# Keys, queries, the recurrent norm's sum, then values: a new sequence in the mixer of a two-layer hybrid network

## What is computed

```python
z = rms_norm(h, mix_pre_g[l]) @ w_in[l]
xr, gr, cq, ckv, kr = jnp.split(z, splits, axis=-1)
y_lru = rglru_group(xr, gr, ...)              # conv, two gates, a scan over tokens, times gelu(gr)
q  = (rms_norm(cq, q_norm_g) @ w_uq)          # 8 heads of 64 + 32 (rope)
kv = (rms_norm(ckv, kv_norm_g) @ w_ukv)       # 8 heads: 64 of key, 64 of value
k_rope = apply_rope(kr, cos[None], sin[None]) # shared by the heads
y_mla = causal_block_attention(qf, kf, v)
y = jnp.concatenate([rms_norm(y_lru, lru_out_g[l]), rms_norm(y_mla, mla_out_g[l])], axis=-1) @ w_out[l]
h = h + rms_norm(y, mix_post_g[l])
```

## Time and profile before

| quantity | value |
|---|---|
| median of 3 executions | 2087.74 us (2084.95 to 2088.3) |
| profiled execution, its own time | 2087.94 us |
| its span, first to last instruction | 2086.1 us |
| PE busy | 2050.4 us, 98% of the span |
| POOL, ACT, DVE busy | 1061.0, 767.5, 729.4 us (51%, 37%, 35%) |
| DMA queue of the weights | 25.9% of 16 engines |
| chain that ended last | PE 89%, POOL 4%, DVE 3%, issue 2%, ACT 1% |
| TensorE clock granted, mean | 0.995 |

### The profile page before, as it was taken

How to read it: one execution, slowest core, us unless ns; L and a number is a source line. 1 busy time by engine, 2 the same in 40 slices (tenths; PEclk the granted TensorE clock), 3 DMA queues, 4 the chain that set the end, 5 groups by cost and what they waited for, 6 DMA issues and landing times.

```text
span 2086.1 us, 39771 instructions
## 1 busy us (share of the span) xinstructions
PE 2050.4 (98%) x16488; PEld 2005.5 (96%) x16488; DVE 729.4 (35%) x1070; ACT 767.5 (37%) x1189; POOL 1061.0 (51%) x1280
## 2 busy tenths in 40 slices
PE   8999999999999999999999999999999999999998
PEld 8999999999888999999999999999998989999997
DVE  5222210478545322220162222104785353222102
ACT  5322232456445322232252222324554453332321
POOL 6555554576205555554375555545662156555541
PEclk9999999999999999999999999999999999999999
DMA  3223232222102322222122233221321123233322
GB/s 140 91 90 90 86 105 84 69 97 81 37 21 62 101 90 90 90 100 88 66 92 91 90 90 94 97 89 64 97 86 31 32 75 97 90 91 100 99 96 69
DMA packets 48274, 174.91 MB, mean 84 GB/s; under 512 B 5168, under 2 KB 9392, under 8 KB 48176
## 3 DMA queue, kind: packets, MB, share of 16 engines
q1 hardware_dynamic: 45792, 170.97, 25.9%
q10 hardware_dynamic: 2384, 2.52, 0.4%
HBM read 171.37 MB, written 2.10 MB: 83 GB/s over the span
## 4 chain that ended last, share of the span: by engine, by line
PE 89%; POOL 4%; DVE 3%; issue 2%; ACT 1%; DMA 0%; ACTq 0%; POOLq 0%; DVEq 0%
PE ps L1381 88%; POOL wlo L593 2%; PE ps L1700 1%; POOL tmp L626 1%; DVE xl L1049 1%; DVE h L1044 1%; DMA h<-in_x 0%; DVE tmp L1038 0%; ACT xh L678 0%; DVE yll L1243 0%; DVE xc L1236 0%; DVE qt L1228 0%; PE ps L1605 0%; ACT whi L654 0%; ACT rs_in L665 0%
## 5 line engine op out<-in xcount | busy, mean ns | idle before, releaser
L593 POOL TENSOR_TENSOR wlo<-raw,whi 128x256 fp32r<-128x256 f32 (+2 forms) x1192 | 993.8, 866 | 912.9 <-ACT whi L654 912.7
L1381 PE MATMUL ps<-xh,whi 128*128 128x264 f32 (+1 forms) x3392 | 725.1, 287 | 20.6 <-DVE xl L1049 11.0
L1381 PE MATMUL ps<-xl,whi 128*128 128x264 f32 (+1 forms) x3392 | 716.4, 284 | 0.0
L1381 PE MATMUL ps<-xh,wlo 128*128 128x264 f32 (+1 forms) x3392 | 715.7, 284 | 0.0
L1381 PEld LDWEIGHTS ps<-xh,whi 128*128 128x128 f32 x3392 | 538.5, 189 | 28.7 <-DVE xl L1049 14.5
L654 ACT ACTIVATE whi<-raw 128x1024 fp32r<-128x1024 f32 (+2 forms) x298 | 334.1, 1122 | 562.9 <-DMA raw<-in_ffn_down 263.1
L1381 PEld LDWEIGHTS ps<-xl,whi 128*128 128x128 f32 x3392 | 537.7, 189 | 0.7
L1381 PEld LDWEIGHTS ps<-xh,wlo 128*128 128x128 f32 x3392 | 537.1, 189 | 0.0
L1381 PE MATMUL ps<-hidh,whi 128*128 128x264 f32 (+1 forms) x1408 | 314.1, 284 | 0.0
L1381 PE MATMUL ps<-hidl,whi 128*128 128x264 f32 (+1 forms) x1408 | 313.0, 283 | 0.0
L1381 PE MATMUL ps<-hidh,wlo 128*128 128x264 f32 (+1 forms) x1408 | 312.8, 283 | 0.0
(11 more groups left out here) (174 smaller groups left out, 1541.4 us busy)
## 6 DMA issues: line engine op xcount, KB each, us to landing
raw<-in_ffn_gate SPq DMA_DIRECT2D x88, 512.0 KB, 3.5
raw<-in_ffn_up SPq DMA_DIRECT2D x88, 512.0 KB, 3.5
raw<-in_ffn_down SPq DMA_DIRECT2D x64, 704.0 KB, 4.1
raw<-in_w_in SPq DMA_DIRECT2D x28, 512.0 KB, 3.5
raw<-in_w_out SPq DMA_DIRECT2D x16, 512.0 KB, 3.5
raw<-in_w_q SPq DMA_DIRECT2D x8, 384.0 KB, 3.1
out_t<-h SPq DMA_DIRECT2D x16, 128.0 KB, 1.7
h<-in_x ACTq DMA_DIRECT2D x2, 528.0 KB, 8.1
```

The lines of the kernel that those rows point to most:

```text
L593: ins = nc.gpsimd.tensor_tensor(wlo[:, r, at], raw[:, r, at], whi[:, r, at].bitcast(F32), ALU.subtract)
L1381: return nc.tensor.matmul(o, w, x, start=start, stop=stop)
```

## The change

Slots and units are numbered anew: keys take slot 15, queries slots 16 to 19, values slot 20. SP loads in that sequence. PE makes the keys after `sel`, then all eight heads, `statl`, and the values last, in units of one, two and two blocks where there were two, two and one. The pair of `statl` is set to 0, so that the values use pairs 1, 2 and 3. Attention waits for heads 4 to 7, `statl` and the first unit of values at its start, for the second unit ahead of item 3's scores and for the third behind them.

The numbering, and the table of pairs:

```diff
-S_XR, S_CQ, S_GATE, S_CKV, S_KR, S_GR, S_V, S_K, S_Q, S_OUT = 0, 4, 7, 8, 10, 11, 15, 16, 17, 21
+S_XR, S_CQ, S_GATE, S_CKV, S_KR, S_GR, S_K, S_Q, S_V, S_OUT = 0, 4, 7, 8, 10, 11, 15, 16, 20, 21
+V_UNITS = ((0,), (1, 2), (3, 4))
...
-                     v=3, k=4, qa=HEADS // 2, statl=1, qb=HEADS // 2, tr=WC, out=DC)
+                     k=4, q=HEADS, statl=1, v=len(V_UNITS), tr=WC, out=DC)
...
-            fixed = {uo: 0, uo + 1: 1, ut: 2, ut + 1: 3, ut + 2: 2, ut + 3: 3, uo + 2: 2}
+            fixed = {U[b, "statl"]: 0, uo: 0, uo + 1: 1, ut: 2, ut + 1: 3, ut + 2: 2, ut + 3: 3, uo + 2: 2}
```

ScalarE: the read-out of `sel` moves ahead of the gelus, that of the values behind `ylh`, and `hi` of slot 19 behind the keys:

```diff
                 for n in (16, 17, 18):
                     hi(s0 + n)
+                act.wait_ge(sel_mm, l + 1)
+                u = U[b, "sel"]
+                nc.scalar.activation(halves(tmp[0], False), unit(u, False), ACT.Copy)\
+                    .then_inc(psum_free[pair_of(u)], 1)
                 for c in range(WC):
...
+                hi(s0 + 19)
                 for c in range(WC):
                     act.wait_ge(y_ready, WC * l + c + 1)
...
                     nc.scalar.activation(ylh[:, c, :], xc[:, c, :], ACT.Copy,
                                          scale=col("lru_out_g", l, c)).then_inc(ylh_ready, 1)
+                for i, blocks in enumerate(V_UNITS):
+                    u = U[b, "v"] + i
+                    if i < 2:
+                        act.wait_ge(v_mm, 2 * l + i + 1)
+                    else:
+                        act.wait_ge(slots_used, slot_used(s0 + S_V))
+                    nc.scalar.activation(vt[:, blocks[0]:blocks[0] + len(blocks), :],
+                                         pair(pair_of(u)).rearrange("p (a b) -> p a b", a=2)[:, 0:len(blocks), :],
+                                         ACT.Copy).then_inc(psum_free[pair_of(u)], 1)
                 for n in (21, 22, 23):
                     hi(s0 + n)
```

VectorE now copies the rope key, multiplies heads 0 and 1, makes the recurrent output times gelu, heads 2 to 4, the sum of squares, heads 5 to 7, the norm of the recurrent output and three low parts `yll`:

```diff
+                queries(0)
+                queries(1)
+                for c in range(WC):
+                    dve.wait_ge(gelu_ready, WC * l + c + 1)
+                    nc.vector.tensor_tensor(xc[:, c, :], xc[:, c, :], gr[:, c, :], ALU.mult)\
+                        .then_inc(y_ready, 1)
+                queries(2)
+                queries(3)
+                queries(4)
+                for c in range(1, WC):
+                    dve.wait_ge(ysq_ready, WC * l + c + 1)
...
+                queries(5)
+                queries(6)
+                queries(7)
                 dve.wait_ge(rs_lru, l + 1)
```

TensorE, at the start of attention and in its loop over items `e`:

```diff
-                last = U[b, "tr"] - 1
-                for u in range(last - 3, last + 1):
+                def read(u):
                     pe.wait_ge(psum_free[pair_of(u)], read_out(u))
+
+                for hd in range(HEADS // 2, HEADS):
+                    read(unit_q(b, hd))
+                read(U[b, "statl"])
+                read(U[b, "v"])
...
+                    if e == NQ - 1:
+                        read(U[b, "v"] + 1)
                     if e < ITEMS:
                         scores(e)
+                    if e == NQ - 1:
+                        read(U[b, "v"] + 2)
```

More of the change, by code:

```diff
@@ L155, in unit_q @@
     def unit_q(b, hd):
-        return U[b, "qa"] + hd if hd < HEADS // 2 else U[b, "qb"] + hd - HEADS // 2
+        return U[b, "q"] + hd
     def pair_of(u):
@@ L862, in mixer @@
                         .then_inc(gelu_ready, 1)
[L863 to L878, removed]
                 for i in range(HEADS // 2):
@@ L1203, in mixer @@
                                                        ALU.mult))
[L1204 to L1219, removed]
                 def queries(hd):
@@ L1230, in queries @@
                         .then_inc(psum_free[pair_of(u)], 1)
-                for hd in range(HEADS // 2):
-                    queries(hd)
+                u = U[b, "sel"]
+                dve.wait_ge(psum_free[pair_of(u)], read_out(u))
+                for i, (p0, p1) in enumerate(((NOPE, P), (0, NOPE))):
+                    nc.vector.tensor_copy(kt_of[i][p0:p1, :, :],
+                                          tmp[0][p0:p1, :].unsqueeze(1).broadcast_to([NOPE, 4, T]))\
+                        .then_inc(krope_ready, 1)
+                queries(0)
[9 more added lines that the diff above has]
+                    dve.wait_ge(ysq_ready, WC * l + c + 1)
+                    if c > 1:
+                        dve.wait_ge(lsum_ready, 3 * l + c - 1)
+                    nc.vector.tensor_tensor(ig[:, 0, :], ig[:, 0, :], ig[:, c, :], ALU.add)\
+                        .then_inc(lsum_ready, 1)
+                queries(5)
+                queries(6)
+                queries(7)
                 dve.wait_ge(rs_lru, l + 1)
@@ L1549, in mixer @@
                 ins.then_inc(sel_mm, 1)
-                n = s0 + S_V
+                n = s0 + S_K
                 slot_in(n)
                 pe.wait_ge(ckvl_ready, KVC * (l + 1))
[L1554 to L1563, removed]
-                            mm(o, ckvh[:, c, t0:t0 + P], wlo[:, r, wv], False, False)
-                            ins = mm(o, ckvl[:, c, t0:t0 + P], whi[:, r, wv], False, c == KVC - 1)
-                    ins.then_inc(v_mm if i < 2 else slots_used, 1)
-                n = s0 + S_K
-                slot_in(n)
                 for i in range(HEADS // 2):
@@ L1584, in mixer @@
                     ins.then_inc(slots_used if hd % 2 else q_mm, 1)
-                    if hd == HEADS // 2 - 1:
-                        pe.wait_ge(lsum_ready, 3 * (l + 1))
-                        us = U[b, "statl"]
-                        partition_sum(us, False, [ig[:, 0, :]], stat_mix)
+                pe.wait_ge(lsum_ready, 3 * (l + 1))
+                partition_sum(U[b, "statl"], False, [ig[:, 0, :]], stat_mix)
+                n = s0 + S_V
+                slot_in(n)
+                r = n % RING
+                for i, blocks in enumerate(V_UNITS):
+                    u = U[b, "v"] + i
+                    unit_free(u)
+                    for q, block in enumerate(blocks):
+                        t0 = block_of(block)[0]
+                        o = pair(pair_of(u))[:, q * 512:(q + 1) * 512]
+                        for c in range(KVC):
+                            wv = slice(c * W, (c + 1) * W)
+                            mm(o, ckvh[:, c, t0:t0 + P], whi[:, r, wv], c == 0, False)
+                            mm(o, ckvh[:, c, t0:t0 + P], wlo[:, r, wv], False, False)
+                            ins = mm(o, ckvl[:, c, t0:t0 + P], whi[:, r, wv], False, c == KVC - 1)
+                    ins.then_inc(v_mm if i < 2 else slots_used, 1)
                 attention(b)
```

16 lines of the change are left out of this document (6 added, 10 removed).

## The result

The changed kernel takes 2101.16 us (median of 8 executions, 2095.62 to 2113.49) against 2088.02 us of the kernel before (8 executions, seven at 2084.95 to 2088.48 us and one at 2103.89); the ratio is 1.0065, with a 95% interval of 1.0043 to 1.0087. The change makes the kernel slower, by more than was forecast: the median lies 2.7 us above the range, and the difference is 13.1 us where 7.5 was forecast. The 8 executions stand in two groups, four at 2095.6 to 2097.8 us with a mean granted clock of 0.991 or 0.992, and four at 2104.5 to 2113.5 us with 0.982 to 0.986. The profiled one is of the upper group: 2109.37 us, span 2107.5 us, clock 0.984. Of all executions in this document one, a slow one of 2494.18 us at a clock of 0.748 in "Denser matmuls in attention", is left out of the numbers.

A forecast was written before the change was run, and what follows sets the result against it. PE, busy 98% of the span, was taken as the bound; one wait removed and two added per layer sum to +7.50 us, so a median of 2095.2 us, with a range of 2092 to 2098 (2089.5 to 2098.5 with rivals).

The forecast's parts named there:

- Part 1, the wait that goes: At attention's first matmul, PE's wait on the last head's read-out goes, a gain of 1.39 + 1.42 = 2.81 us.
- Part 2, the wait ahead of head 0: PE waits for ACT to read out the first key unit and free its PSUM pair: 2.54 and 2.64 us.
- Part 3, the wait at attention's second step: Three roundings behind the last values' read-out make ACT later for attention: 1.68 us in layer 0, 3.45 in layer 1.
- The sum of the waits: Over both layers, -2.81 + 2.54 + 2.64 + 1.68 + 3.45 = +7.50 us.
- the first rival: Both new waits are real and the clock halves at layer 1's attention start, +2.6 us: 2097.8; chance 0.15.
- PE was fully busy up to the stall: Argument against a clock fall at layer 1's attention start: unlike at the seam, PE has no idle time before it.
- The milder rivals: ACT reaches the keys in time, 2090.0, chance 0.07; attention's start has slack, 2090.1, 0.07; only the gain, 2084.9, 0.03.

The follow-up runs named there:

- Denser matmuls in attention: Changed kernel with 12 useless matmuls ahead of the scores of items 4 to 11 in both layers; 5 executions, 2108.66 to 2120.06 us, ratio 1.0115.
- part 3 undone: Changed kernel with slots 21 and 22 rounded behind slot 20, slot 23 ahead of the last value unit; 2093.15 us, and 2091.93 us once more.
- filler: Changed kernel with useless matmuls ahead of item 0's transposes, 18 in layer 0 and 58 in layer 1; 2095.66 us, ratio 1.0034.
- the wait doubled: Changed kernel with each of the three roundings ahead of attention done twice; 2103.18 us, ratio 1.0078.
- both undone: Changed kernel with three key units read out ahead of the gelus and slots 21 to 23 rounded earlier, TensorE's new sequence kept; 2086.59 us, ratio 0.9990.
- the old sequence: Kernel before, with ScalarE rounding slots 21 to 23 only once the last head has been read out; 2095.73 us, ratio 1.0024.

## Why the prediction was wrong

**Part 1, the wait that goes: right.** The wait on `qt` is gone in both layers, and values and `statl` cover the last head.

**Part 2, the wait ahead of head 0: right in mechanism and place, 0.2 to 0.4 us too long in each layer.** Forecast 2.54 and 2.64 us; from the keys' 5.90 us of work the gaps are 509.66 - 507.36 = 2.30 and 1567.30 - 1565.01 = 2.29 us. ACT's read-out started at 508.31 (508.37 forecast). The table load's new place brought no drain (504.87 to 506.16, 1.29 us, where it was 504.43 to 505.72). Undoing this part took the lower group from 2097.2 to 2090.65 us, 6.5 us, where the waits make 4.6; a short fall of the clock at the wait costs 1.5 us where a trace has it. The seven traces with this wait (the changed kernel, its repeat, both runs with part 3 undone, and the runs with filler, with the wait doubled and with denser matmuls) have it at 5 of their 14 waits, so about 1 us per execution, an estimate, and some 0.8 us of the 6.5 stay unexplained. **That term was missing.**

**Part 3, the wait at attention's second step: right in mechanism, 0.4 to 0.5 us too long in each layer,** since the last values were read out 0.1 us behind attention's start (0.35 forecast) and the roundings took 2.84 us to the next instruction (3.05 forecast). PE stood 1.1 us and 3.4 us there. Against the kernel before, ACT came to attention 1.2 and 3.0 us later, where 1.68 and 3.45 was forecast.

**The sum of the waits** looks better than it is. Forecast were +7.5 us and the lower group is +8.3. But the waits in the trace make only +6.2: the stretch from keys to attention is 2.46 and 2.33 us over PE's 31.32 us of work, less the 2.81 lost before, and 1.10 and 3.10 us come at attention's second step. That waits forecast 1.3 us too long nearly met the lower group is luck: short falls of the clock, which the sum left out, fill the gap. The kernels built to take parts away bear out the mechanism as differences from the lower group of before measured beside them: +1.8, -2.9 and +2.0 us where the waits alone gave +2.4, -2.4 and +2.2, and +5.8 us over the changed kernel's lower group for the doubled roundings, where 6.0 was expected.

**The step that failed is the first rival**, "both new waits are real and the clock falls too". It was given 0.15 and 2.6 us, once, in layer 1, with "8 matmuls in 2 us where the full clock had 19" and the six microseconds of the seam as its length. The sum itself put the clock at nothing. The runs showed a long fall in 11 of 20 executions, in layer 0 in both traces that caught one, over 37.5 us, at a price of 15.4 us (medians of the two groups, 2112.6 and 2097.2). Two errors are in it. The length was taken from the seam, 6.8 us there (661.0 to 667.8), where long matmuls of the feed-forward block follow; in attention it was anything from 3.4 to 37.5 us. And the weighing against it, "PE was fully busy up to the stall", took a high busy share as a sign that the clock was safe. In layer 1, where the rival was placed, the clock fell in both traces although PE had been busy up to the stall, for 3.4 us, at some 1.5 us where the rival gave 2.6; and the fall that cost most came in layer 0, behind matmuls of 16 columns that count as fully busy, at a wait of 1.1 us that the rival did not price. That the kernel before has a long fall in 16 of 101 executions could not be seen in the three that were shown, so 2088 us was no fixed mark either.

**The milder rivals** fell: ACT is not in time for the keys, and attention's start has no slack.

**What stays open** is what sets off a fall and what makes one long and the next one short. The excess over the waits is shown to be time at half clock. Idle time at attention's start goes with more long falls in two comparisons (11 of 20 against 0 of 24 with the roundings earlier; 6 of 12 against 16 of 101 in the old sequence) and, less firmly, in a third (2 of 12 with filler). It is neither enough nor needed: with head 0's wait gone, the share is 4 of 12 with it and 4 of 12 with at most 1.4 us of it; more of it does not raise the share (3 of 12); and falls come without any, two at attention's start and four at its end in the traces. The falls at attention's start that came with a wait, wait and length in us: 1.0 us and 6.8, 1.1 and 37.5 (twice), 1.1 and 17.1, 2.0 and 20.5, 3.4 and 3.4 (twice), 3.4 and 13.7, 4.4 and 6.8, 6.7 and 6.8. That attention's light load holds the clock down is a guess; falls of 3.4 us within attention are against it.

## What to carry to other kernels

A reordering on the bottleneck engine has to be followed to the engine that reads its output: here TensorE's sequence was better by 2.8 us by the waits that it took away, and both losses came from ScalarE's sequence, one from a reader that was late for a PSUM pair, one from three roundings that had lost their cover; moved, they gave 0.24% over the kernel before. And a fall of the clock cost more here, up to 15.4 us, than the wait at which it came: look for the granted clock beside each wait, don't take a busy share of 100% as a sign that the clock is safe, and look at every execution's clock before a median is taken for the kernel's time.

## What the runs showed of the hardware that was not expected

The granted clock fell to 0.50 at standstills of 2.1 us within otherwise dense work (for 3.4 us each, 22 matmuls in 4 us where 35 are usual) and of 1.1 us at attention's start (for 37.5 us), and in six places with no standstill at all, all in attention, where PE counts as fully busy: two near its start (27.3 and 3.4 us) and four at its end (3.4 us each, in the runs with part 3 undone and with both undone). In attention a fall lasted anything from 3.4 to 37.5 us; at the seam behind the mixer it lasted 3.4 or 6.8 us. The Trainium skill's page "TensorE: Matmul & The Clock Gate", section "HAM oscillation — how this bites in real kernels", ties the fall to gaps in which TensorE is idle; the traces here agree where a standstill is at hand, and the six falls without one go beyond it. A switch of ACT's tables took 1.29 or 1.30 us from the load's start to the next instruction's in the traces (504.87 to 506.16 in the changed kernel).
